# Two transformer blocks on one core: the weight sums of the seven-product down units, added by DMA instead of by VectorE, with the units at places 2, 4, 6, 8

## What is computed

```python
def _swiglu_ffn(x, g_norm, w_gate_up, w_down):
    h = _rms_norm(x, g_norm)
    gate, up = jnp.split(h @ w_gate_up, 2, axis=-1)
    return (jax.nn.silu(gate) * up) @ w_down      # (256 x 2816) @ (2816 x 1024)

def first_block(x, ...):
    for layer in range(2):
        x = x + mixer(x)                           # gmlp, then chunked attention
        x = x + _swiglu_ffn(x, ...)
    return _rms_norm(x, final_norm)
```

## Time and profile before

| | |
|---|---|
| median of 3 runs | 1216.2 us (1215.86 to 1216.25) |
| span of the profiled execution | 1214.1 us (2.1 us under the median; no time of its own is recorded for it) |
| TensorE busy | 1205.5 us, 99% of the span |
| VectorE busy | 903.9 us, 74% |
| ScalarE busy | 671.1 us, 55% |
| GpSimd busy | 51.3 us, 4% |
| DMA | 220.40 MB, mean 182 GB/s |

### The profile page before, as it was taken

How to read it: one execution, slowest core, us unless ns; L and a number is a source line. 1 busy time by engine, 2 the same in 40 slices (tenths; PEclk the granted TensorE clock), 3 DMA queues, 4 the chain that set the end, 5 groups by cost and what they waited for, 6 DMA issues and landing times.

```text
span 1214.1 us, 17930 instructions
## 1 busy us (share of the span) xinstructions
PE 1205.5 (99%) x7099; PEld 1048.0 (86%) x7099; DVE 903.9 (74%) x1105; ACT 671.1 (55%) x807; POOL 51.3 (4%) x101
## 2 busy tenths in 40 slices
PE   9999999999999999999999999999999999999998
PEld 7888888888899888888888889999888888999986
DVE  5566465568886685566988986988887998698886
ACT  7655354445466664444648556555655755566553
POOL 2000000000010000000010020000001011000000
PEclk9999999999999999999999999999999999999999
DMA  9644645545654335554555454455574435555550
GB/s 349 232 164 168 223 147 200 194 163 196 243 191 166 131 141 206 207 179 168 193 214 174 139 177 161 152 205 174 174 262 161 140 107 184 191 179 180 196 196 35
DMA packets 32568, 220.40 MB, mean 182 GB/s; under 512 B 3888, under 2 KB 4048, under 8 KB 6768
## 3 DMA queue, kind: packets, MB, share of 16 engines
q1 hardware_dynamic: 29888, 212.33, 49.3%
q0 software_dynamic: 1664, 5.41, 1.3%
q10 hardware_dynamic: 944, 1.64, 0.4%
HBM read 218.31 MB, written 1.05 MB: 181 GB/s over the span
## 4 chain that ended last, share of the span: by engine, by line
PE 92%; DVE 6%; DMA 1%; issue 0%; POOL 0%; ACT 0%; ACTq 0%; POOLq 0%; DVEq 0%
PE acc L1850 20%; PE acc L1852 20%; PE acc L1851 20%; PE tb L1878 3%; PE tb L2521 3%; PE tb L2520 3%; PE acc L2520 3%; PE acc L2521 3%; PE tb L2518 3%; PE acc L2518 3%; DVE cacc L1534 3%; DVE wlo L1143 1%; PE acc L2158 1%; PE acc L2160 1%; PE acc L2161 1%; PE tb L1850 1%
## 5 line engine op out<-in xcount | busy, mean ns | idle before, releaser
L1143 DVE TENSOR_TENSOR wlo<-raw,whi 128x2048 fp32r<-128x2048 f32 x184 | 417.3, 2287 | 131.8 <-ACT whi L592 131.8
L592 ACT ACTIVATE whi<-raw 128x2048 fp32r<-128x2048 f32 (+1 forms) x198 | 368.4, 1882 | 56.5 <-PE acc L1852 43.9
L1850 PE MATMUL acc<-whi,xth 128*128 128x512 f32 x704 | 279.8, 397 | 0.6 <-DVE xtl L1241 0.5
L1852 PE MATMUL acc<-whi,xtl 128*128 128x512 f32 x704 | 274.7, 390 | 0.0
L1851 PE MATMUL acc<-wlo,xth 128*128 128x512 f32 x704 | 274.3, 390 | 0.0
L1850 PE MATMUL acc<-whi,yth 128*128 128x512 f32 (+1 forms) x428 | 169.0, 395 | 0.0
L1852 PE MATMUL acc<-whi,ytl 128*128 128x512 f32 (+1 forms) x428 | 166.6, 389 | 0.0
L1851 PE MATMUL acc<-wlo,yth 128*128 128x512 f32 (+1 forms) x428 | 166.4, 389 | 0.0
L1850 PEld LDWEIGHTS acc<-whi,xth 128*128 128x128 f32 x704 | 132.3, 188 | 28.0 <-DVE wlo L1232 1.3
L1852 PEld LDWEIGHTS acc<-whi,xtl 128*128 128x128 f32 x704 | 132.2, 188 | 28.1
L1851 PEld LDWEIGHTS acc<-wlo,xth 128*128 128x128 f32 x704 | 132.4, 188 | 25.7
(11 more groups left out here) (407 smaller groups left out, 1919.3 us busy)
## 6 DMA issues: line engine op xcount, KB each, us to landing
raw<-in_stream SPq DMA_DIRECT2D x200, 1024.0 KB, 5.0
rb<-in_rel_rows POOLq DMA_DIRECT2D x8, 256.0 KB, 2.9
x<-in_x_in ACTq DMA_DIRECT2D x4, 256.0 KB, 7.4
raw<-in_stream SPq DMA_DIRECT2D x2, 512.0 KB, 9.3
gs_sb<-in_gs_row POOLq DMA_DIRECT2D x1, 1024.0 KB, 7.6
frow<-in_fin_row POOLq DMA_DIRECT2D x2, 512.0 KB, 6.0
raw<-in_stream SPq DMA_DIRECT2D x2, 256.0 KB, 7.0
ws_sb<-in_ws_t POOLq DMA_DIRECT2D x1, 512.0 KB, 7.7
```

The lines of the kernel that those rows point to most:

```text
L592: act.activation(whi[:, s, c0:UNIT], raw[:, s, c0:UNIT], ACT.Copy).then_inc(hi_ready, 1)
L1143: dve.tensor_tensor(wlo[:, s, :], raw[:, s, :], whi[:, s, :], ALU.subtract).then_inc(lo_ready, 1)
L1850: pe.matmul(o, xh, wh, start=first, stop=False)
L1852: return pe.matmul(o, xl, wh, start=False, stop=last)
```

## The change

The weight sums of the eight seven-product units of the first block are no longer made by VectorE from `raw`. GpSimd issues five DMA transfers for each unit: two plain copies from `stream` in DRAM into the sums' buffer, two transfers from `stream` that add to what is there, and one from one half of the buffer that adds to the other half. There is a wait for the landing after the second and after the fourth, and ahead of the first. The signs of the scheme are changed, so that all four sums are plain sums; the activations' sums and `fold_sums` follow with changed signs at the same count of instructions. `sums_hi` waits for the fifth transfer's landing. The four seven units of a stage stand at places 2, 4, 6, 8 (before: 2, 4, 6, 7), and so the order of the weights is the natural one. `fold_sums` moves one place later. The two feed-forwards of the second block keep VectorE's sums.

```diff
-SEVEN_POS = (2, 4, 6, 7)
-DOWN_ORDER = (0, 1, 2, 3, 4, 5, 6, 8, 7, 9, 10)
+SEVEN_POS = (2, 4, 6, 8)
+DOWN_ORDER = tuple(range(CTF))
...
+            def weight_sums(e):
+
+                for i in range(SEVEN):
+                    w, b = w_sums(e, i)[0], stream[down_at(e) + SEVEN_POS[i]]
+                    b12, b22 = b[:, 0:512], b[:, 1024:1536]
+                    done = 80 * (SEVEN * e + i)
+                    if done:
+                        pool.wait_ge(wsum_landed, done)
+                    if i == 0:
+                        pool.wait_ge(n_lo, 4 * (2 * e + 1) + 4)
+                        pool.wait_ge(n_sq, 2 * STATS[2 * e + 1] + 2)
+                    else:
+                        pool.wait_ge(unit_used, down_at(e) + (SEVEN_POS[i - 2] + 1 if i >= 2 else 0))
+                    pool.dma_start(w[:, 0:1536], b[:, 512:2048]).then_inc(wsum_landed, 16)
+                    pool.dma_start(w[:, 1536:2048], b22).then_inc(wsum_landed, 16)
+                    pool.wait_ge(wsum_landed, done + 32)
+                    pool.dma_start(w[:, 0:1024].rearrange("p (a c) -> p a c", c=512),
+                                   b12.unsqueeze(1).to_broadcast([P, 2, 512]), accum_op=ALU.add).then_inc(wsum_landed, 16)
+                    pool.dma_start(w[:, 1024:1536], b22, accum_op=ALU.add).then_inc(wsum_landed, 16)
+                    pool.wait_ge(wsum_landed, done + 64)
+                    pool.dma_start(w[:, 1024:2048].rearrange("p (a c) -> p a c", c=512),
+                                   w[:, 0:512].unsqueeze(1).to_broadcast([P, 2, 512]),
+                                   accum_op=ALU.add).then_inc(wsum_landed, 16)
+
             root(1)
+            weight_sums(0)
             root(2)
...
             root(3)
+            weight_sums(1)
             pool.wait_ge(unit_used, U_DOWN1 + SEVEN_POS[-1] + 1)
...
             def sums_hi(e, i):
                 f, h, _ = w_sums(e, i)
-                act.wait_ge(lo_ready, down_at(e) + sevens(e)[i] + 1)
+                if e < 2:
+                    act.wait_ge(wsum_landed, 80 * (SEVEN * e + i + 1))
+                else:
+                    act.wait_ge(lo_ready, down_at(e) + sevens(e)[i] + 1)
                 act.activation(h[:, :], f[:, :], ACT.Copy).then_inc(side_hi, 1)
...
                 lo(U0 + 2 * CTF + 2)
-                sums(e, 0)
                 keep(CTF - 1)
                 for j in range(1, CTF):
                     lo(U0 + 2 * CTF + j + 2)
-                    if j in (1, 3, 5, 6):
-                        sums_lo(e, (1, 3, 5, 6).index(j))
-                    if j + 2 in SEVEN_POS:
-                        sums(e, SEVEN_POS.index(j + 2))
-                    if j == CTF - 3:
+                    if j + 1 in SEVEN_POS:
+                        sums_lo(e, SEVEN_POS.index(j + 1))
+                    if j == CTF - 2:
                         fold_sums(e)
```

More of the change, by code:

```diff
@@ L249, in two_blocks_kernel @@
         hi_ready, lo_ready, unit_used = sem("hi_ready"), sem("lo_ready"), sem("unit_used")
+        wsum_landed = sem("weight_sums_landed")
         m0_done, out_group = sem("m0_done"), sem("out_group")
@@ L258, in two_blocks_kernel @@
             sem(n) for n in ("consts_loaded", "consts_made", "made"))
-        n_add, n_tr, n_gm, n_hi, n_lo, n_sq, n_ms, n_r = (
-            sem("norm_" + n) for n in ("added", "transposed", "gained", "hi", "lo", "squared", "meaned", "rms"))
+        n_add, n_tr, n_gm, n_hi, n_lo, n_sq, n_r = (
+            sem("norm_" + n) for n in ("added", "transposed", "gained", "hi", "lo", "squared", "rms"))
         x2_z, x2_hi, x2_lo = sem("second_x_scaled"), sem("second_x_hi"), sem("second_x_lo")
@@ L263, in two_blocks_kernel @@
         f_ms, f_rt = sem("final_meaned"), sem("final_rms")
-        side_made, x_r2 = sem("side_made"), sem("mix_own_rms")
-        a_ev, a_vsq, a_vsum, a_ms, a_r, a_vn, a_sp, a_spc, a_y, y_banks, a_hi, a_lo = (
-            sem("gmlp_" + n) for n in ("act", "v_squared", "v_summed", "v_meaned", "v_rms", "v_normed", "spatial",
+        side_made, pool_step = sem("side_made"), sem("pool_own_step")
+        a_ev, a_vsq, a_vsum, a_r, a_vn, a_sp, a_spc, a_y, y_banks, a_hi, a_lo = (
+            sem("gmlp_" + n) for n in ("act", "v_squared", "v_summed", "v_rms", "v_normed", "spatial",
                                        "spatial_kept", "gated", "turned_then_sums_done", "hi", "lo"))
@@ L283, in two_blocks_kernel @@
             sem("conv_" + n) for n in ("padded", "sigmoid", "gated", "transposed", "kept", "tap"))
-        x_ltr, x_bn, x_ag, x_lms, x_lr, x_nrm, x_btr, x_sl = (
-            sem("conv_ln_" + n) for n in ("transposed", "stats", "mean", "var", "rstd", "normed", "back", "silu"))
+        x_ltr, x_bn, x_ag, x_lr, x_nrm, x_btr, x_sl = (
+            sem("conv_ln_" + n) for n in ("transposed", "stats", "mean", "rstd", "normed", "back", "silu"))
         x_ev = sem("mix_kept")
@@ L389, in made_count @@
         def made_count(e, n):
-            return 2 + 36 * min(e, 2) + 22 * max(e - 2, 0) + n
+            return 2 + 24 * min(e, 2) + 22 * max(e - 2, 0) + n
         def is_seven(U):
@@ L459, in _, with then_wait @@
                                pattern=[[-GCH, P // GCH], [0, GCH]], channel_multiplier=1).then_inc(consts_made, 1)
+            steps = [0]
+            def then_wait(op):
+                steps[0] += 1
+                op.then_inc(pool_step, 1)
+                pool.wait_ge(pool_step, steps[0])
             def root(r, outer=None):
                 pool.wait_ge(n_sq, 2 * r + 2)
-                pool.tensor_scalar(ssq(r, 0, 2), ssq(r, 0, 2), 1.0 / D, EPS, ALU.mult, ALU.add).then_inc(n_ms, 1)
-                pool.wait_ge(n_ms, r + 1)
+                then_wait(pool.tensor_scalar(ssq(r, 0, 2), ssq(r, 0, 2), 1.0 / D, EPS, ALU.mult, ALU.add))
                 two = stat[:, 2 * r:2 * r + 2]
@@ L468, in root @@
                 if outer is not None:
-                    last.then_inc(x_r2, 1)
-                    pool.wait_ge(x_r2, 1)
+                    then_wait(last)
                     last = pool.tensor_tensor(two, two, stat[:, 2 * outer:2 * outer + 2], ALU.mult)
@@ L767, in glu @@
                 for j in range(1, CTF):
[L768 removed]
+                    if j == CTF - 1:
                         first_sum(e)
                     hi(U0 + 2 * CTF + j + 2)
[L771 to L772 removed]
+                    if j + 1 in SEVEN_POS:
+                        sums_hi(e, SEVEN_POS.index(j + 1))
             glu(0, U_GLU0, C_GLU0, 1, PAIR_GLU0)
@@ L1140, in lo @@
                 if is_seven(U):
-                    dve.tensor_tensor(wlo[:, s, 512:UNIT], raw[:, s, 512:UNIT], whi[:, s, 512:UNIT], ALU.subtract)
+                    o = dve.tensor_tensor(wlo[:, s, 512:UNIT], raw[:, s, 512:UNIT], whi[:, s, 512:UNIT], ALU.subtract)
+                    if U < U_MIX:
+                        o.then_inc(lo_ready, 1)
                 else:
@@ L1148, in sums @@
                 s, n = U % SLOTS, made_count(e, 4 * len(sevens(e)) + 3 * i)
+                assert e >= 2
                 b12, b11, b22, b21 = (raw[:, s, 512 * b:512 * b + 512] for b in range(4))
@@ L1898, in seven @@
                 w = [slice(512 * b, 512 * b + 512) for b in range(4)]
+                t1, t3, t2, t4 = (w[b] for b in ((0, 1, 3, 2) if e < 2 else range(4)))
                 pe.wait_ge(lo_ready, U + j + 1)
@@ L1914, in p4 @@
                 def p4():
-                    return split3(c21[:, :], yth3[:, y + 1, m1], ytl3[:, y + 1, m1], wh[:, w[3]], wl[:, w[3]], False, False)
+                    return split3(c21[:, :], yth3[:, y + 1, m1], ytl3[:, y + 1, m1], wh[:, t4], wl[:, t4], False, False)
                 def p5():
-                    split3(b5, sum_h[:, s1], sum_l[:, s1], wh[:, w[0]], wl[:, w[0]], first, last)
+                    split3(b5, sum_h[:, s1], sum_l[:, s1], wh[:, t1], wl[:, t1], first, last)
                 def p7():
-                    return split3(b7, yth3[:, y, m1], ytl3[:, y, m1], wh[:, w[1]], wl[:, w[1]], first, last)
+                    return split3(b7, yth3[:, y, m1], ytl3[:, y, m1], wh[:, t3], wl[:, t3], first, last)
                 def p6():
-                    return split3(b6, sum_h[:, s2], sum_l[:, s2], wh[:, w[2]], wl[:, w[2]], first, last)
+                    return split3(b6, sum_h[:, s2], sum_l[:, s2], wh[:, t2], wl[:, t2], first, last)
                 p1()
```

20 lines of the change are left out of this document (9 added, 11 removed).

## The result

The changed kernel takes 1293.67 us (median of 4 runs, 1291.51 to 1295.20), the kernel before 1216.03: a ratio of 1.064 (95% interval 1.062 to 1.065), 77.6 us slower. It was forecast slower, at 1262.8 within 1218 to 1312: right in direction, mechanism and range, 31 us short in size. The four runs of the changed kernel lie within 3.7 us, so a few microseconds beside them say nothing.

A forecast was written before the change was run, and what follows sets the result against it. TensorE was taken to bound both down stages without a gap. Two stages at 23.3 us of stall add 46.6 to the 1214.1 us span, and 2.1 for the median gives 1262.8 us, range 1218 to 1312.

The forecast's parts named there:

- What bounds the kernel, and that nothing could be won: Both down stages: TensorE works without a gap, so taking work from VectorE can only be free or cost.
- The terms at zero: Down stages: VectorE's 16 fewer additions, later fold, seam (0.2 us at most), SyncE's loads and GpSimd's queue, all priced at nothing.
- The chain as the mechanism: Down stages: three fillings in turn stall TensorE at places 4, 6, 8; 3L - 39.7, 23.3 us a stage.
- L: Time of one filling's three steps: 6.6 us fixed, 10.1 transfer at half a copy's rate, 4.3 stream; 21 us.
- rival 3: Fillings: additions slower than half rate or heavy contention; L = 28.5 gives 1308 us, L = 33 gives 1335; chance 0.21.
- A: First step of a filling: copies 786 + 262 KB, 2.88 us of transfer.
- B: Second step of a filling: adds 524 + 262 KB, 4.32 us of transfer at half a copy's rate.
- C: Third step of a filling: adds 524 KB, 2.88 us of transfer at half a copy's rate.
- The stream's share: SyncE's loads beside a filling: three units' loads take 8.6 us, half falling where data moves, 4.3 us more.
- The clock: TensorE behind a stall: half clock, matmuls 0.43 us apart for a while; not in the sum, left to the range.
- Rival 1: Fillings: additions at the copy's rate, L from 12.5 to 17, 3 to 23 us over both stages; chance 0.20.
- Rival 2: Down stages: the chain hides, L at or under 12.4 us, at most 2.4 us, 1216 to 1218; chance 0.12.

The follow-up runs named there:

- experiment 7: Changed kernel with only each stage's first sum made by DMA, VectorE making the other three: 1215.89 us against 1216.14 for the kernel before, ratio 0.9999.
- experiment 1: Kernel before with only the order changed (places 2, 4, 6, 8, later fold), VectorE still making the sums: 1215.76 us against 1216.14, ratio 0.9998.
- experiment 4: Changed kernel with only the sums of places 2 and 4 filled in each stage, places 6 and 8 reusing what is left: 1234.79 us.
- experiment 5: Kernel without the network, a filling's steps by themselves, on idle engines and beside loads or VectorE: 17.8 us together alone.
- experiment 9: Kernel without the network, copies and additions of several sizes, and B beside loads: within SBUF, 512 KB copy 2.9 us, addition 4.6.
- experiment 8: Changed kernel with SyncE loading only the first 128 columns of each unit, a sixteenth of the stream: 1261.71 us.
- experiment 6: Changed kernel with matmuls of zeros put in TensorE's waits for the weight sum: 1294.34 us.
- run 32: Not a run's label: words of "plain copies run 32 us faster", said of the changed kernel with plain copies instead of adding, 1262.0 us.
- experiment 3: Changed kernel with the same five transfers a filling as plain copies, without adding: 1262.0 us.

## Why the prediction was right, and where it was short

**What bounds the kernel, and that nothing could be won:** shown. Taking 5.3 us from VectorE (experiment 7) moved nothing; the 19.8 us of the whole change were never tried without the chain. **The terms at zero:** shown for order, fold and seam (experiment 1).

**The chain as the mechanism:** shown. Six waits at the three places named, ended by `wsum_l`; with the second and third filling gone, they go (experiment 4). The formula holds: the measured 3L of 75.7 and 73.8 gives 3L - 39.7 = 36.0 and 34.1. To it come 0.8 us a stage from the stage's start to the first issue (277.65 to 278.41), which I had at zero, and 1.9 and 2.2 of low clock: 75.8 for both stages. The trace has 76.1, by the first GpSimd instruction behind the second stage (705.92 against 629.83 with the order alone); 0.4 of it stand between the two runs before the first down stage already (277.65 against 277.26).

**The price of a filling** is the step that was mis-sized, L = 21 against a mean of 24.9, worth 2 x 3 x 3.9 = 23 us. The mean is just inside the forecast's band (L from 17 to 25), but L = 25 gives 1287 us by the sum; the time is inside the range because the range reached up toward rival 3 (L = 28.5).

By its terms, from the DMA queues in the window of each filling of the first stage. Queue q0 carries GpSimd's transfers, q1 SyncE's loads; the last number is the time of the packets as a share of the 16 engines' time:

```profile
q1 hardware_dynamic: 578, 4.20, 48.8%
q0 software_dynamic: 912, 2.36, 39.7%
...
q0 software_dynamic: 912, 2.36, 43.8%
q1 hardware_dynamic: 288, 2.10, 24.6%
...
q0 software_dynamic: 912, 2.36, 46.4%
q1 hardware_dynamic: 288, 2.10, 26.8%
```

The filling's own packets take 10.8, 10.9 and 11.0 us of 27.1, 24.9 and 23.6, where I had 10.1; on idle engines (experiment 5) they take 10.8 of 17.8 (A 2.9, B 4.9, C 3.1, where I had 2.88, 4.32 and 2.88), which leaves 7.0 for the fixed parts, where I had 6.6. So the steps alone, 16.7, were nearly right, and so was the half rate for an addition on the engines (experiment 9; with plain copies the packets of the first three fillings take 6.1 to 7.2 us). The Trainium skill (Collectives: The Full Stack, section "The bandwidth ceiling: the fold count and why AG ≠ RS ≠ AR") gives half of a copy's rate for the additions of a ring of several cores, and the trace agrees with it for the packets' time (1.29 against 2.75 us). It doesn't hold for the time to landing: from 512 KB to 1 MB a copy within SBUF grows by 1.7 us and an addition by 2.4.

The stream's share, taken as 4.3 us (half of three loads), is what failed. Over the steps alone (17.8) a filling took 5.8 to 9.3 us more, 7.1 in the mean. The working took the loads as three, spread evenly, also over the fixed parts of the steps. The packets of the stream take 6.1 and 6.3 us in the second and third filling, two whole loads, and 13.2 us in the first, four loads. They are not spread evenly: the `lo` that releases a load stands on VectorE behind `wsum_l` of the last filling. In the timeline of VectorE in the changed kernel

```profile
307.17 2.29 DVE L1200 TENSOR_TENSOR wsum_l<-wsum,wsum_h 128x2048 fp32r<-128x2048 f32 x1 [12.63 <-ACT wsum_h L631]
309.38 1.75 DVE L1175 TENSOR_TENSOR wlo<-raw,whi 128x1536 fp32r<-128x1536 f32 x1
311.05 2.29 DVE L1179 TENSOR_TENSOR wlo<-raw,whi 128x2048 fp32r<-128x2048 f32 x1
```

two loads are let go at 311.1 and 313.3, and step B starts at 311.08: it took 14.1 us. SyncE issues them just then:

```profile
L432 SPq DMA_DIRECT2D raw<-in_stream x2: 332/332/333, 311.3 to 313.5; - x2
```

In the third filling it is the same (loads at 336.2 and 338.4, B from 336.08, 12.9 us). In the first, three of the four loads come at 288.5, 292.3 and 294.5 and fall mostly into step C, which took 12.6 us. So this filling is the longest, and place 4, where I had 1.7 us, waits 8.1 and 7.3 us, while the 10.8 at places 6 and 8 were nearly met. A step beside two loads is 10.1 to 12.5 us on otherwise idle engines (experiment 5), so up to 2 us of the 14.1 stay open. That timing decides the share is argued from these rows; no run moved the loads. And not all of it is bytes: with a sixteenth of the stream a filling still took 0.9 to 2.5 us more than 17.8 (experiment 8).

**The clock** was left to the range. TensorE was idle for 7.3 to 12.1 us, then matmuls started 0.43 us apart, the level of 1.2 GHz, at a granted clock of 0.50. The Trainium skill (TensorE: Matmul & The Clock Gate, section "HAM oscillation — how this bites in real kernels") has TensorE at half of its clock after waits for DMA, and the trace agrees. Of the 14.7 us of busy time that came with it, only 1.9 and 2.2 reach the end (experiment 6).

**Rival 1**, additions at the copy's rate, fell: plain copies run 32 us faster (experiment 3), and an addition's packets take up to twice a copy's time (experiment 9). **Rival 2**, no change, needed L of at most 12.4; even idle engines need 17.8. The estimate of 11.4 us from the Trainium skill (DMA: Bandwidth & Descriptors, section "Anatomy of one DMA — SWDGE (gpsimd) path") fell: a plain copy of 512 KB from DRAM took 4.0 to 5.1 us here, and 3.2 by that page's formula. **Rival 3** was half right: the traffic beside a filling cost more than I had, but not the additions themselves.

**Left open:** 1.8 of the 77.9 us between the spans (1291.9 against 1214.0 with the order alone) lie behind the last VectorE instruction: 3.2 us from its end to the span's end with the order alone, 5.0 in the changed kernel. It was also near 5 us with plain copies and with the thin stream, and 3.3 in the kernel with 20 such transfers instead of 40 (experiment 4). Its cause wasn't looked for.

## What to carry to other kernels

Before work is moved from a busy but hidden engine to DMA, look at whether the engine that bounds the stage ever waits; if it doesn't, the move can only cost. A chain of dependent transfers is priced as links times (fixed cost plus transfer plus all the traffic beside it), and held against the spacing of the times at which its results are wanted, not against the total DMA load. Where a transfer has its whole buffer life ahead of it, as the first sum here, it is free.

## What the runs showed of the hardware that was not expected

- On idle engines an addition by DMA lands only 1.0 to 1.7 us after its copy would at 512 KB and 2.3 to 2.5 us at 1 MB, though within SBUF its packets take about twice the copy's time on the engines (2.75 against 1.29 us, 5.18 against 2.73).
- A load of 256 KB beside an adding step delays it by 1.5 to 2.1 us, nearly as much as one of 1 MB (2.2); a second and a third 1 MB load add 2.5 each.
- GpSimd's issue of an adding transfer lasts 1.2 us in two of the three shapes here, against 0.7 for its copying twin.
- A clock that falls during a wait costs almost nothing while a chain elsewhere sets the pace: 14.7 us more of busy time, about 4 us at the end.
